# The end of a mixer + MoE decode kernel: norm rows loaded with h, the last down product by column halves, the mean from an accumulated output, sample rows over 128 partitions

## The chip, the cores and the metric

The kernel runs on 1 core of one Trainium2 chip. The metric is the device time of one execution in microseconds (us). Before the change it is 1081.07 us, the median of 3 runs (1079.88 to 1082.58).

## What is computed

One decoder layer in fp32 on 512 prompt tokens and 8 sample tokens, 520 in all, each of 1024 features. A three-branch token mixer and a first LayerNorm give `h`. Then, cut from the reference:

```
f = sum over e of gates[:, e] * ((silu(h @ w_gate[e]) * (h @ w_up[e])) @ w_down[e])   # 16 experts, top 2 per token
y = layer_norm(ALPHA * h + f, ln2_g, ln2_b)
layer_norm(x) = (x - mean) * rsqrt(mean((x - mean)^2) + 1e-5) * g + b                 # over the 1024 features
```

Each token has two experts with weights that add up to one. The outputs are `y` for the prompt, `y` for the samples, and the convolution states, which are done long before the end.

## The kernel before

The five engines run programs written by hand, each in the order in which it is written, and meet at semaphores. Nothing is reordered by a scheduler. The names below are those of the code: `pe` is TensorE, `act` ScalarE, `dve` VectorE, `pool` GpSimd, `sp` the queue on SyncE from which most DMAs are issued. On each engine `settle()` is a wait of the engine for its own last result.

The mixer takes the first 740 us. Then the 16 experts follow, step `m` = 0 to 15 (in the order of `TURN`), each on up to 96 tokens (`C`) that are gathered to one tile. fp32 matrices are split into a rounded part and a remainder, so that each product takes three passes: `act` writes the rounded weights into `ring` (L764), `dve` subtracts them to get the remainder (`low_parts`, L1497), and `pe` multiplies hi by hi, hi by lo, lo by hi (`product`, L1076). A step of `pe` is: gate product, up product (both to 512 columns), and the down product of the expert before (to 1024 columns in two halves of 512, each in a PSUM bank of its own), 24 matmuls of 512 columns each. A step of `dve` holds the 12 remainders of the three matrices and four smaller things. After each down product `act` copies 96 rows of 1024 from PSUM to `y_out` (`rows_out`, L805) and `sp` stores them in the DRAM table `y_rows` (`store`, L444).

Where a token's two rows stand in that table comes from the routing. `find_slots` (L1569) works it out for each of the two choices, on tiles of 128 partitions x 5 token blocks: block 0 to 3 are the prompt, block 4 holds the 8 samples, so that 8 partitions of it are in use. It runs on `dve` at the ends of the steps m = 13 and m = 14. `order_slots` (L1580) orders the two, in step m = 15, in the middle of the remainders of the up matrix.

The end goes through these steps:

- `load_back` (L446): when the down product of m = 13 is done, `sp` loads `h` back from DRAM (`h_back`). The rows of gain and bias of the last norm (`load_rows`, `ln2_rows`) are loaded after the store of m = 14.
- `fetch` (L600): `pool` gathers for each of the five blocks the row of the earlier expert (`y_a`), as soon as the slots are known and 12 experts are stored. After the last store has landed, `sp` signals `y_read` (L517), and `pool` gathers the rows of the later expert (`y_b`).
- `partials` (L1597) on `dve`: y_a = y_a * weight + h_back, five blocks, after `h_back` and the norm's rows have landed.
- `summed_up(b)` (L1625): y_a = y_b * weight + y_a (L1629), then `bn_stats` on two halves (L1631) and `bn_aggr` (L1633) for mean and variance.
- `act` takes the root of the variance, 128 x 1 (L862).
- `normalise(b)` (L1635): (y_a - mean) * g (L1638), a reciprocal of the root (L1640), and times that plus the bias row (L1642). Then `sp` stores the block (L523).

`dve` runs `summed_up(0)`, and then for b = 1 to 4 `summed_up(b)` and `normalise(b - 1)`, and `normalise(4)`. The last product, `down_last` (L1086), takes the four chunks of 128 rows one after the other and in each both column halves, so that both halves end together.

Of the kernel before, what the change touches and what calls it, by code (L numbers as in the profile page):

```python
# [30 lines left out]
P = 128  # L31
# [82 lines left out]
def build(nc, x_prompt, x_sample, state_conv_a, state_conv_b, w_in, conv_a_w, w_a_out, conv_b_w, conv_b_bias,  # L114
# [16 lines left out]
    with ExitStack() as ctx:  # L131
# [61 lines left out]
        h_back = place("h_back", "X_HI", [P, NTB, D], plus=NTB * D * 4)  # L193
        y_b = place("y_b", "Q_HI", [P, NTB, D])
        ln2_rows = place("ln2_rows", "Q_HI", [P, 2, D], plus=NTB * D * 4)
# [32 lines left out]
        s_max, s_sum, s_w1, s_w2, s_ps, s_t, s_slot, s_slot2 = (sb(f"s{i}", [P, NTB]) for i in range(8))  # L228
# [9 lines left out]
        hs = place("hs", "tail_b", [C, D])  # L238
        y_out = place("y_out", "b_pad", [C, D], plus=6 * NTB * E * 4)
# [15 lines left out]
        stats = sb("stats", [P, 2, 2, 6])  # L255
# [8 lines left out]
        const_ready, spatial_masked, pool_chain = sem("const_ready"), sem("spatial_masked"), sem("pool_chain")  # L264
# [11 lines left out]
        mean_rounded, x_mean_ready, z_ready, sq_ready, h_white = (sem(n) for n in ("mean_rounded", "x_mean_ready", "z_ready", "sq_ready", "h_white"))  # L276
        wo_in = [sem(f"wo_in{j}") for j in range(4)]
        wo_centred, rw_b_ready, rw_ready, b_ready = sem("wo_centred"), sem("rw_b_ready"), sem("rw_ready"), sem("b_ready")
        tok_var, tok_std, diag_ready, r_spread = sem("tok_var"), sem("tok_std"), sem("diag_ready"), sem("r_spread")
        lg_transposed, table_ready = sem("lg_transposed"), sem("table_ready")  # L280
# [20 lines left out]
        lg_turned, lg_ready = sem("lg_turned"), sem("lg_ready")  # L301
        loads_begun, gathers_begun = sem("loads_begun"), sem("gathers_begun")
# [5 lines left out]
        fin_out = [sem("fin_out0"), sem("fin_out1")]  # L308

        MATRICES = ("gate", "up", "down")  # L310

        class Pass:


            def __init__(self, tag):
# [10 lines left out]
                self.stored = sem(tag + "stored")  # L326
# [8 lines left out]
                "meanB": (centred, 2), "varB": (std_ready, 2), "meanX": (x_mean_ready, 1), "biasL": (b_ready, 1),  # L335
# [47 lines left out]
        def _(sp):  # L383
# [4 lines left out]
            def load(slot, n, view, col):  # L388
                sp.wait_ge(w_split, n * 2 + 2)
                sp.sem_inc(loads_begun, 1)  # L390
                sp.dma_start(raw[:, slot], view[:, :, bass.ds(col, P)]).then_inc(raw_in[slot], 16)
# [59 lines left out]
            def load_rows():  # L451
# [414 lines left out]
        def _(pe):  # L866
# [271 lines left out]
            with pe.Else():  # L1138
                pe.nop()
# [535 lines left out]
```

## Time and profile before

| | us |
|---|---|
| median of 3 runs | 1081.07 |
| the profiled execution's own time | 1081.94 |
| its span in the trace | 1079.9 |
| PE busy | 997.7 (92%) |
| DVE busy | 807.4 (75%) |
| ACT busy | 472.1 (44%) |
| POOL busy | 344.5 (32%) |
| end of the last matmul | 1040.6 |
| the first `y_b` is used | 1051.18 |

The busy times are of the whole span and say little of its end: the last 39 us, 3.6% of the span, hold no matmul. TensorE's granted clock is at full speed up to its last matmul. The trace counts from the start of the profiled execution, whose own time is 2.0 us longer than its span.

### The profile page before, as it was taken

The page shows a single profiled execution, that of the slowest core. Times are in us where ns is not written, and L with a number is a line of the kernel's source. Part 1 is how long each engine was busy: PE and PEld are TensorE (multiplying, and loading weights), DVE is VectorE, ACT ScalarE, POOL GpSimd, SP SyncE. Part 2 cuts the span into 40 slices and gives each one's busy share as a digit, 9 for nine tenths or more (in the row PEclk, how much of TensorE's full clock was granted, in tenths as well). Part 3 has the DMA queues.
Part 4 walks back from the last instruction along what each step waited for, and adds up shares of the span by engine and source line. Part 5 has one row for each costly group of instructions (what it writes and reads, how often), then busy time and mean ns, then how long its engine had stood idle before and what let it go on. Part 6 is the DMA issues. An engine that isn't in the chain of part 4 may idle for free.

```text
span 1079.9 us, 19395 instructions
## 1 busy us (share of the span) xinstructions
PE 997.7 (92%) x7175; PEld 902.5 (84%) x7175; DVE 807.4 (75%) x986; ACT 472.1 (44%) x657; POOL 344.5 (32%) x268
## 2 busy tenths in 40 slices
PE   6999999999999899999999998986999999999950
PEld 5999999999999798999999998964677777777630
DVE  2398889888898976744335596147889898989969
ACT  3222322322322144334442322245787878787820
POOL 2444444444544241445445443410200000000060
PEclk9999999999999899999999998996999999999985
DMA  7423332332332221332334524457999999999562
GB/s 202 121 86 92 97 89 86 97 94 81 97 96 61 78 78 49 97 114 79 97 97 156 175 78 156 157 198 269 337 371 377 390 385 389 385 389 344 186 200 108
DMA packets 162375, 189.91 MB, mean 176 GB/s; under 512 B 5875, under 2 KB 113395, under 8 KB 162316
## 3 DMA queue, kind: packets, MB, share of 16 engines
q1 hardware_dynamic: 155819, 177.46, 48.4%
q0 software_dynamic: 3008, 10.55, 3.1%
q10 hardware_dynamic: 3505, 1.36, 0.5%
q8 instruction: 24, 0.39, 0.2%
q14 instruction: 19, 0.16, 0.0%
HBM read 178.57 MB, written 11.76 MB: 176 GB/s over the span
## 4 chain that ended last, share of the span: by engine, by line
PE 51%; issue 28%; POOL 12%; DVE 4%; DMA 2%; ACT 2%; POOLq 0%; DVEq 0%; ACTq 0%
PE pr L915 26%; PE pr L1076 14%; POOL w_lo L546 10%; PE work L1076 7%; DMA hs<-h_rows,ids 2%; PE work L1062 1%; POOL y_a L603 1%; PE work L985 1%; DVE stats L1631 1%; DVE y_a L1629 1%; ACT h_f L773 1%; DVE y_b L1638 1%; PE work L1037 1%; DMA y_b<-y_rows,slot_b 0%; PE pr L1093 0%
## 5 line engine op out<-in xcount | busy, mean ns | idle before, releaser
L546 POOL TENSOR_TENSOR w_lo<-raw,w_hi 128x512 fp32r<-128x512 f32 x208 | 281.6, 1373 | 365.3 <-ACT w_hi L631 365.3
L915 PE MATMUL pr<-x_hi,w_hi 128*128 128x260 f32 x1280 | 259.7, 284 | 3.1 <-POOL w_lo L546 3.1
L915 PE MATMUL pr<-x_hi,w_lo 128*128 128x260 f32 x1280 | 259.0, 284 | 0.0
L915 PE MATMUL pr<-x_lo,w_hi 128*128 128x260 f32 x1280 | 258.9, 284 | 0.0
L635 ACT ACTIVATE ev<-pr 128x520 f32<-128x520 f32 x96 | 58.2, 606 | 389.2 <-PE pr L915 389.2
L915 PEld LDWEIGHTS pr<-x_hi,w_hi 128*128 128x128 f32 x1280 | 199.0, 190 | 3.5 <-DVE x_lo L1183 3.3
L915 PEld LDWEIGHTS pr<-x_hi,w_lo 128*128 128x128 f32 x1280 | 198.5, 190 | 0.0
L915 PEld LDWEIGHTS pr<-x_lo,w_hi 128*128 128x128 f32 x1280 | 198.2, 190 | 0.0
L1235 DVE SCALAR_TENSOR_TENSOR work<-b_pad,par,work 128x512 f32<-128x512 f32 x224 | 148.1, 744 | 0.0
L631 ACT ACTIVATE w_hi<-raw 128x512 fp32r<-128x512 f32 x208 | 118.9, 622 | 5.5 <-DMA raw<-in_w_in_dram 3.2
L1076 PE MATMUL pr<-ring,hs_hi 128*96 128x512 f32 x256 | 103.0, 403 | 4.1 <-DVE hs_lo L1503 2.0
L582 POOL DMA_INDIRECT hs<-h_rows,ids x16 | 20.1, 1259 | 256.2 <-DVE ids L1491 215.9
L1076 PE MATMUL pr<-ring,hs_lo 128*96 128x512 f32 x256 | 101.5, 396 | 0.0
L1497 DVE TENSOR_TENSOR w_up_lo<-w_up,ring 128x1024 fp32r<-128x1024 f32 x64 | 75.5, 1221 | 21.9 <-ACT ring L764 21.8
L1497 DVE TENSOR_TENSOR w_gate_lo<-w_gate,ring 128x1024 fp32r<-128x1024 f32 x64 | 75.2, 1214 | 3.7 <-ACT ring L764 3.5
L764 ACT ACTIVATE ring<-w_gate 128x1024 fp32r<-128x1024 f32 x64 | 67.4, 1060 | 21.1 <-PE pr L1076 12.1
L1497 DVE TENSOR_TENSOR w_down_lo<-w_down,ring 128x1024 fp32r<-128x1024 f32 x64 | 75.2, 1216 | 0.0
L1290 DVE TENSOR_TENSOR ev<-ev,ev 128x520 f32<-128x520 f32 x16 | 11.9, 743 | 79.9 <-ACT ev L635 79.9
L764 ACT ACTIVATE ring<-w_down 128x1024 fp32r<-128x1024 f32 x64 | 65.7, 1054 | 8.1 <-PE pr L1076 8.1
L764 ACT ACTIVATE ring<-w_up 128x1024 fp32r<-128x1024 f32 x64 | 62.4, 1047 | 3.4 <-PE pr L1076 3.4
L1076 PEld LDWEIGHTS pr<-ring,hs_hi 128*96 128x96 f32 x256 | 41.8, 163 | 22.6 <-DVE hs_lo L1503 2.3
L1076 PEld LDWEIGHTS pr<-ring,hs_lo 128*96 128x96 f32 x256 | 41.8, 163 | 18.3
(279 smaller groups left out, 1675.9 us busy)
## 6 DMA issues: line engine op xcount, KB each, us to landing
raw<-in_w_in_dram SPq DMA_DIRECT2D x80, 512.0 KB, 3.7
w_gate<-in_expert_w_gate_dram SPq DMA_DIRECT2D x16, 2048.0 KB, 14.6
w_up<-in_expert_w_up_dram SPq DMA_DIRECT2D x16, 2048.0 KB, 13.7
w_down<-in_expert_w_down_dram SPq DMA_DIRECT2D x16, 2048.0 KB, 13.3
y_rows<-y_out SPq DMA_DIRECT2D x16, 384.0 KB
raw<-in_w_a_out_dram SPq DMA_DIRECT2D x8, 512.0 KB, 3.6
raw<-in_w_c_out_dram SPq DMA_DIRECT2D x8, 512.0 KB, 3.6
raw<-in_w_b_out_dram SPq DMA_DIRECT2D x8, 512.0 KB, 3.6
```

The source lines that it names most:

```text
L546: pool.tensor_tensor(w_lo[:, slot, k], raw[:, slot, k], w_hi[:, slot, k].bitcast(F32), ALU.subtract).then_inc(w_split, 1)
L582: pool.indirect_dma_start(out=hs[:], out_offset=None, in_=h_rows, in_offset=bass.IndirectOffsetOnAxis(ap=ids[:, m % 2:m % 2 + 1], axis=0)) ...
L603: pool.indirect_dma_start(out=dst[0:n, b, :], out_offset=None, in_=table, in_offset=bass.IndirectOffsetOnAxis(ap=slot[0:n, b:b + 1], axis= ...
L631: act.activation(w_hi[:, slot, k], raw[:, slot, k], ACT.Copy).then_inc(w_rounded, 1)
L635: act.activation(out, src[:, :, 0:HALF], func).then_inc(evacuated, 1)
L764: act.activation(rounded(kind, i, last), chunk(kind, s, i), ACT.Copy).then_inc(ps.hi[kind], 1)
L773: act.activation(h_f[:, k, :], h_f[:, k, :], ACT.Identity, scale=par[:, k * NROWS + R_L1G:k * NROWS + R_L1G + 1], bias=par[:, k * NROWS + ...
L915: mm = pe.matmul(pr[slot][:, h, 0:HALF], w[:, slot, k, :], x[:, k, h * HALF:(h + 1) * HALF], start=(k == 0 and w is w_hi and x is hi), sto ...
L1076: mm = pe.matmul(out(h), x[:, k, :], w[:, cols], start=(k == 0 and x is hi and w is w_hi_i), stop=(k == k_of * CH - 1 and x is lo))
L1235: do(dve.scalar_tensor_tensor(acc, b_pad[:, k:k + TP], col(j, R_CONVB + k), acc, ALU.mult, ALU.add))
L1290: do(dve.tensor_tensor(gate[:], gate[:], prod[:], ALU.mult))
L1497: dve.tensor_tensor(chunk(kind, s, i, w_e_lo), chunk(kind, s, i), rounded(kind, i, last).bitcast(F32), ALU.subtract).then_inc(ps.lo_dve[ki ...
```

## The change

1. **Norm rows.** `ln2_rows` moves to the memory of expert slot 1, beside `h_back`, and is loaded in `load_back`. For the samples a second copy of gain and bias is laid out by 16 small loads of 16 partitions x 64.
2. **Slots.** `find_slots` works out both choices together and runs once, at m = 13; a compare with a table `kc` and one sum replace a loop over the passes. `order_slots` moves from m = 15 to the end of m = 14 and also prepares the 5 columns `s_own` for the samples.
3. **Samples over 128 partitions.** The 8 rows of 1024 are treated as 128 rows of 64. `pool` builds two masks after its last gather of tokens; `pe` spreads `s_own` from 8 to 128 partitions by a matmul in the middle of the down product of m = 14; `spread_samples` on `dve` copies it and makes indices, after its last remainders; each gather of samples waits for that. Mean and variance of a sample are put together over 16 partitions by two matmuls with `block_mean`.
4. **Last down product by halves.** All four chunks of columns 0 to 511 first, then 512 to 1023. `act` copies each half as it is done to a buffer of its own, `sp` stores each by itself. `pool` waits for the stores itself, without `y_read`.
5. **Mean and variance.** L1744 writes the sum of its output to `agg` as it goes (`accum_out`), a small multiply turns it into minus the mean, and `act` squares (`Square` with that as bias, also summed as it goes) and takes the root. `bn_stats` and `bn_aggr` are gone. The samples come between the prompt's blocks, and prompt block 3 is the last.

The rest are semaphores that are merged with others. The core of the diff:

```diff
@@ sp: load_back, the last stores
-                sp.dma_start(h_back[0:TS, 4, :], h_rows[TP:T, :]).then_inc(back_in, 16)
+                sp.dma_start(sh_back, h_rows[TP:T, :].rearrange("s (c f) -> (s c) f", f=CS)).then_inc(back_in, 16)
+                for i, row in enumerate((ln2_g, ln2_b)):
+                    sp.dma_start(ln2_rows[:, i, :], row[0].partition_broadcast(P)).then_inc(ln_in, 16)
+                    for s in range(TS):
+                        k = P // TS
+                        sp.dma_start(sln2[s * k:(s + 1) * k, i, :], row[0].rearrange("(c f) -> c f", f=CS)).then_inc(ln_in, 16)
+            def store_last(ps, q, row0):
+                x = E - 1
+                sp.wait_ge(ps.half_ready, q + 1)
+                sp.dma_start(y_rows[bass.ds(x * C + row0, C), 0:D // 2], y_last[:, 0:D // 2]).then_inc(ps.half_stored, 16)
+                sp.wait_ge(ps.y_ready, q * E + (E + 1))
+                sp.dma_start(y_rows[bass.ds(x * C + row0, C), D // 2:D], y_last[:, D // 2:D]).then_inc(ps.stored, 16)
@@ pool: after the last token gather
+            def fetch_samples(dst, which, landed, table):
+                pool.indirect_dma_start(out=dst, out_offset=None, in_=table.rearrange("r (c f) -> (r c) f", f=CS),
+                                        in_offset=bass.IndirectOffsetOnAxis(ap=s_idx[:, which:which + 1], axis=0)).then_inc(landed[4], 16)
             fetch(y_a, slot_early, y_a_in, y_rows[0:EARLY * C, :])
+            pool.wait_ge(sample_dve, 2)
+            fetch_samples(sy_a, 0, y_a_in, y_rows[0:EARLY * C, :])
...
             with pool.Else():
-                pool.wait_ge(y_read, 1)
+                pool.wait_ge(first.half_stored, 16)
+                pool.wait_ge(first.stored, 16 * (E + 1))
                 fetch(y_b, slot_b, y_b_in, y_rows[0:E * C, :])
+                fetch_samples(sy_b, 2, y_b_in, y_rows[0:E * C, :])
@@ act
+            def last_rows_out(ps, t):
+                act.wait_ge(ps.done["down"], t * CH + CH + 2)
+                act.activation(y_last[:, 0:512], work[0][0:C, 0, :], ACT.Copy).then_inc(ps.half_ready, 1)
+                act.wait_ge(ps.done["down"], t * CH + 2 * CH)
+                act.wait_ge(ps.stored, t * 16 + 16)
+                act.activation(y_last[:, 512:1024], work[0][0:C, 1, :], ACT.Copy).then_inc(ps.y_ready, 1)
+            def deviation(b):
+                s = b % 2
+                act.wait_ge(var_ready, b + 1)
+                act.activation(pr[0][:], y_a[:, b, :].rearrange("p (h n) -> p h n", h=2), ACT.Square, bias=agg[:, s, 1:2],
+                               accum_out=agg[:, s, 2:3]).then_inc(std2_ready, 1)
+                act.wait_ge(std2_ready, 2 * b + 1)
+                act.activation(agg[:, s, 3:4], agg[:, s, 2:3], ACT.Sqrt, scale=1.0 / D, bias=eps_t[:, 1:2]).then_inc(std2_ready, 1)
@@ dve: expert_pass
-                    if ps is first and m == E - 1:
-                        order_slots()
...
                     if ps is first and m == 13:
-                        find_slots(oh1, s_slot)
+                        find_slots()
                     if ps is first and m == 14:
-                        find_slots(oh2, s_slot2)
+                        order_slots()
@@ dve: the end
-                step(dve.scalar_tensor_tensor(y_a[0:n, b, :], y_b[0:n, b, :], s_wb[0:n, b:b + 1], y_a[0:n, b, :], ALU.mult, ALU.add))
-                for h in range(2):
-                    do(dve.bn_stats(stats[0:n, s, h, :], y_a[0:n, b, h * 512:(h + 1) * 512]))
+                step(dve.scalar_tensor_tensor(y_a[:, b, :], y_b[:, b, :], s_wb[:, b:b + 1], y_a[:, b, :], ALU.mult, ALU.add,
+                                              accum_out=agg[:, s, 0:1]))
+                do(dve.tensor_scalar(agg[:, s, 1:2], agg[:, s, 0:1], -1.0 / D, None, ALU.mult), to_var)
```

Where the change moves instructions, at three places. First `dve` in the last expert step (m = 15), before; the rows ahead of it are `find_slots`, which ends in eleven instructions on 128x5, each waiting for the one before. `w_up_lo` are remainders of the up matrix, `s_...` the small tiles of the slots:

```order
L1578 TENSOR_TENSOR s_144<-s_144,s_142 128x5
L1497 TENSOR_TENSOR w_up_lo_86<-w_up_77,ring 128x1024 x2
L1582 TENSOR_TENSOR s_142<-s_143,s_144 128x5
L1583 TENSOR_TENSOR s_137<-s_140,s_142 128x5
...
L1594 TENSOR_SCALAR s_142<-s_142 128x5
L1595 CAST slot_early<-s_142 128x5
L1497 TENSOR_TENSOR w_up_lo_86<-w_up_77,ring 128x1024 x2
L1497 TENSOR_TENSOR w_down_lo_91<-w_down_82,ring 128x1024 x2
L1517 TENSOR_TENSOR u_lo<-pr,u_hi 128x384
```

and the same place now (`s_own`, `s_pos` belong to the slots, too):

```order
L1588 TENSOR_TENSOR w_gate_lo_83<-w_gate_74,ring 128x1024 x2
L1679 TENSOR_TENSOR s_151<-s_pair 128x5
...
L1697 CAST slot_early<-s_pos 128x5
L1698 TENSOR_TENSOR s_own<-s_pos,id_cols 8x1
L1588 TENSOR_TENSOR w_up_lo_86<-w_up_77,ring 128x1024 x4
L1588 TENSOR_TENSOR w_down_lo_91<-w_down_82,ring 128x1024 x2
L1608 TENSOR_TENSOR u_lo<-pr,u_hi 128x384
```

The slots' order now takes the place of the second `find_slots`, and the four remainders of the up matrix follow each other with nothing between them.

Second the queue of `sp`, from the load of `h` to the last store, before:

```order
L448 DMA h_back<-h_rows 128x4x1024
L449 DMA h_back<-h_rows 8x1024
L444 DMA y_rows<-y_out 96x1024
L452 DMA ln_rows<-in_ln_g_dram 128x1024
L453 DMA ln_rows<-in_ln_b_dram 128x1024
```

and now (the 16x64 loads are the samples' copy of gain and bias):

```order
L459 DMA h_back<-h_rows 128x4x1024
L460 DMA h_back<-h_rows 128x64
L462 DMA ln_rows<-in_ln_g_dram 128x1024
L465 DMA h_back<-in_ln_g_dram 16x64 x8
L462 DMA ln_rows<-in_ln_b_dram 128x1024
L465 DMA h_back<-in_ln_b_dram 16x64 x8
L455 DMA y_rows<-y_out 96x1024
```

Eighteen loads stand ahead of the store of m = 14 that stood behind it or were not there.

Third the end on `dve`, one block in the middle, before:

```order
L1629 SCALAR_TENSOR_TENSOR y_a<-y_b,s_138,y_a 128x1024
L1631 BN_STATS stats<-y_a 128x6 x2
L1633 BN_AGGR agg<-stats 128x2
L1638 SCALAR_TENSOR_TENSOR y_b<-y_a,agg,ln_rows 128x1024
L1640 RECIPROCAL agg<-agg 128x1
L1642 SCALAR_TENSOR_TENSOR y_a<-y_b,agg,ln_rows 128x1024
```

and the last rows now (`s_agg` and 128x64 are the samples):

```order
L1764 SCALAR_TENSOR_TENSOR y_a,s_agg<-y_b,s_spread,y_a 128x64
L1744 SCALAR_TENSOR_TENSOR y_a,agg<-y_b,s_147,y_a 128x1024
L1746 TENSOR_SCALAR agg<-agg 128x1
L1751 SCALAR_TENSOR_TENSOR y_b<-y_a,agg,ln_rows 128x1024
L1753 RECIPROCAL agg<-agg 128x1
L1755 SCALAR_TENSOR_TENSOR y_a<-y_b,agg,ln_rows 128x1024
L1769 SCALAR_TENSOR_TENSOR y_b<-y_a,s_agg,h_back 128x64
L1771 RECIPROCAL s_agg<-s_agg 128x1
L1773 SCALAR_TENSOR_TENSOR y_a<-y_b,s_agg,h_back 128x64
L1751 SCALAR_TENSOR_TENSOR y_b<-y_a,agg,ln_rows 128x1024
```

and on `act`, where `pr` is only a place to write the squares:

```order
L923 ACTIVATE pr,agg<-y_a,agg 128x1024
L926 ACT_TABLE_LOAD
L926 ACTIVATE agg<-agg,eps_t 128x1
L923 ACTIVATE pr,agg<-y_a,agg 128x1024
L926 ACTIVATE agg<-agg,eps_t 128x1
```

Two passes over 512 columns each left `dve`, one over 1024 came to `act`, and the table load that stood ahead of all roots stands behind the first square.

## Rows read from the trace of the kernel before

**Rows 1.** Busy time by stretch: from:to us, length, busy us and count per engine, PEclk, DMA.
```profile
1040.62:1051.18 10.56, 0.00 (x0) 0.00 (x0) 6.11 (x5) 2.30 (x2) 4.47 (x4) 0.74 0.55 174
1051.18:1077.72 26.54, 0.00 (x0) 0.00 (x0) 26.02 (x35) 1.47 (x5) 1.74 (x2) 0.50 0.34 130
```
**Rows 2.** Timeline of DVE from 1051 us: start, us, engine, line, operation, tiles.
```profile
1051.18 1.28 DVE L1629 SCALAR_TENSOR_TENSOR y_a<-y_b,s,y_a 128x1024 f32<-128x1024 f32 x1 [0.81 <-DMA y_b<-y_rows,slot_b]
1052.50 1.29 DVE L1631 BATCH_NORM_STATS2 stats<-y_a 128x6 f32<-128x512 f32 x2
1053.82 0.21 DVE L1633 BATCH_NORM_AGGREGATE agg<-stats 128x2 f32<-128x12 f32 x1
1053.95 1.24 DVE L1629 SCALAR_TENSOR_TENSOR y_a<-y_b,s,y_a 128x1024 f32<-128x1024 f32 x1
...
1056.67 1.23 DVE L1638 SCALAR_TENSOR_TENSOR y_b<-y_a,agg,ln_rows 128x1024 f32<-128x1024 f32 x1
...
1059.21 1.28 DVE L1629 SCALAR_TENSOR_TENSOR y_a<-y_b,s,y_a 128x1024 f32<-128x1024 f32 x1
...
1076.45 1.27 DVE L1642 SCALAR_TENSOR_TENSOR y_a<-y_b,agg,ln_rows 8x1024 f32<-8x1024 f32 x1
```
**Rows 3.** Timeline of POOL from 1031 us.
```profile
1031.07 6.38 POOL L603 DMA_INDIRECT y_a<-y_rows,slot_early  x1 [0.30 <-issue]
1045.80 1.77 POOL L603 DMA_INDIRECT y_b<-y_rows,slot_b  x1 [8.35 <-SPq L517]
1047.88 0.94 POOL L603 DMA_INDIRECT y_b<-y_rows,slot_b  x1 [0.30 <-issue]
```
**Rows 4.** Timeline of SP's queue.
```profile
963.19 2.37 SPq L444 DMA_DIRECT2D y_rows<-y_out  x1
...
1017.12 0.89 SPq L449 DMA_DIRECT2D h_back<-h_rows  x1
...
1041.70 0.35 SPq L444 DMA_DIRECT2D y_rows<-y_out  x1
```
**Rows 5.** Waits of SP's queue from 980 us: total us, times, longest.
```profile
SPq L513 <- DMA y_rows<-y_out: 3.3, 1, 3.3
```
**Rows 6.** Timeline of PE, last expert's product.
```profile
1028.88 0.47 PE L1076 MATMUL work<-ring,u_hi 128*96 128x512 f32 x1 [0.87 <-DVE u_lo L1517]
...
1040.22 0.40 PE L1076 MATMUL work<-ring,u_lo_last 128*96 128x512 f32 x1
```
**Rows 7.** Waits from 980 us: total us, times, longest.
```profile
PE pr L1076 <- DVE w_up_lo L1497: 1.1, 1, 1.1
```
**Rows 8.** Timeline of DVE around the slots, and its last remainders.
```profile
1016.58 0.23 DVE L1570 TENSOR_TENSOR router<-router,e_off 128x80 f32<-128x80 f32 x1
...
1019.64 2.36 DVE L1497 TENSOR_TENSOR w_up_lo<-w_up,ring 128x1024 fp32r<-128x1024 f32 x2
1021.92 0.15 DVE L1582 TENSOR_TENSOR s<-s,s 128x5 f32<-128x5 f32 x1
...
1023.73 2.36 DVE L1497 TENSOR_TENSOR w_up_lo<-w_up,ring 128x1024 fp32r<-128x1024 f32 x2
...
1034.35 2.35 DVE L1497 TENSOR_TENSOR w_down_lo<-w_down,ring 128x1024 fp32r<-128x1024 f32 x2
```
**Rows 9.** Timeline of ACT from 1040 us.
```profile
1040.65 1.02 ACT L805 ACTIVATE y_out<-work 96x1024 f32<-96x1024 f32 x1 [4.53 <-PE work L1076]
1044.74 1.28 ACT L862 ACT_TABLE_LOAD   x1 [3.07 <-issue]
1054.07 0.29 ACT L862 ACTIVATE agg<-agg,eps_t 128x1 f32<-128x1 f32 x1 [8.04 <-DVE agg L1633]
```
**Rows 10.** Groups of ACT's instructions: busy us, mean ns, idle before.
```profile
L756 ACT ACTIVATE ev<-m 128x520 f32<-128x520 f32 x8 | 5.1, 638 | 41.7 <-DVE m L1394 41.7
```
**Rows 11.** DMA issues: KB each, median us to landing.
```profile
out_dram<-y_a SPq DMA_DIRECT2D x4, 512.0 KB, 2.6
```
**Rows 12.** Tile `y_b`: from issue to landing.
```profile
DMA to landing us min/median/max: 5.0/5.4/6.0
```

More of the change, by code:

```diff
@@ L842, in expert_pass @@
                 rows_out(ps, t - 1)
[L843 removed]
+                last_rows_out(ps, t)
             act.sem_inc(first.silu_ready, 1)
@@ L1087, in down_last @@
                 pe.wait_ge(ps.u_lo_ready, t + 1)
-                product(ps, "down", 0, t, u_hi_last, u_lo_last, lambda h: work[0][0:C, h, :], 2, last=True)
+                for h in range(2):
+                    for k in range(CH):
+                        if h == 0:
+                            pe.wait_ge(ps.lo_dve["down"], t * CH + (k + 1))
+                        cols = slice(h * 512, (h + 1) * 512)
+                        w_lo_k, w_hi_k = chunk("down", 0, k, w_e_lo), rounded("down", k, True)
+                        for x, w in ((u_hi_last, w_hi_k), (u_hi_last, w_lo_k), (u_lo_last, w_hi_k)):
+                            mm = pe.matmul(work[0][0:C, h, :], x[:, k, :], w[:, cols], start=(k == 0 and x is u_hi_last and w is w_hi_k),
+                                           stop=(k == CH - 1 and x is u_lo_last))
+                    mm.then_inc(ps.done["down"], 2)
             def turn_u(ps, t):
@@ L1120, in expert_pass @@
                 turn_u(ps, t)
+                if ps is first:
+                    pe.wait_ge(const_ready, 6)
+                    pe.wait_ge(sample_dve, 1)
+                    pe.matmul(pr[1][:, 1, 8:13], spread[:], s_own[:], start=True, stop=True).then_inc(sample_mm, 1)
                 down(ps, (E - 2) % 3, t - 1, chunks=(2, 3))
@@ new lines, in order_slots, with spread_samples @@
+                do(dve.tensor_copy(slot_early[:], s_pos[:, 0, :]), to_slots)
+                do(dve.tensor_tensor(s_own[:, 0:1], s_pos[0:TS, 0, 4:5], own, ALU.subtract), Tally(dve, sample_dve, 0))
+                last[0] = chain
+            def spread_samples():
+                last[0] = chain
+                dve.wait_ge(sample_mm, 1)
+                step(dve.tensor_copy(s_spread[:], pr[1][:, 1, 8:13]))
+                dve.scalar_tensor_tensor(s_idx[:], s_spread[:, 0:3], float(P // TS), id_cols[:, 0, 1:2].to_broadcast([P, 3]), ALU.mult,
+                                         ALU.add).then_inc(sample_dve, 1)
@@ new lines, in summed_up, with normalise @@
+                do(dve.tensor_scalar(agg[:, s, 1:2], agg[:, s, 0:1], -1.0 / D, None, ALU.mult), to_var)
+            def normalise(b):
+                s = b % 2
+                to_var.wait(0 if b == 3 else 1)
+                do(dve.scalar_tensor_tensor(y_b[:, b, :], y_a[:, b, :], agg[:, s, 1:2], ln2_rows[:, 0, :], ALU.add, ALU.mult))
+                dve.wait_ge(std2_ready, 2 * b + 2)
+                do(dve.reciprocal(agg[:, s, 3:4], agg[:, s, 3:4]))
+                settle()
+                do(dve.scalar_tensor_tensor(y_a[:, b, :], y_b[:, b, :], agg[:, s, 3:4], ln2_rows[:, 1, :], ALU.mult, ALU.add), to_fin)
@@ L1644, in _ @@
             last[0] = chain
             summed_up(0)
-            for b in range(1, NTB):
-                summed_up(b)
-                normalise(b - 1)
-            normalise(NTB - 1)
+            summed_up(1)
+            normalise(0)
+            summed_up(2)
+            normalise(1)
+            dve.wait_ge(y_b_in[4], 16)
+            do(dve.scalar_tensor_tensor(sy_a, sy_b, s_spread[:, 4:5], sy_a, ALU.mult, ALU.add, accum_out=s_agg[:, 0:1]), Tally(dve, sample_dve, 2))
+            last[0] = chain
```

231 lines of the change are left out of this document (142 added, 89 removed).

## The prediction, made before the changed kernel was run

> **What bounds the end of the kernel now.** I read the page's chain of waits first, then the busy time by stretch, then the timelines of DVE, POOL, SP and PE over the last 60 us. The change touches nothing that is on the chain before the last two expert steps, so the first 1015 us stay. After that the chain has four pieces.
>
> (a) PE runs to 1040.62, where its last matmul ends [rows 6]. It is almost full, but it waits twice in the last expert step, 1.1 us for a remainder of the up matrix [rows 7] and 0.87 us for `u_lo` [rows 6]. Both come from DVE, and in front of both DVE has worked on slots: 3.06 us of `find_slots` from 1016.58 to 1019.64, and 1.81 us of `order_slots` from 1021.92 to 1023.73 [rows 8].
>
> (b) Then there is a relay with almost no work in it, 10.56 us without a matmul [rows 1]. ACT copies the last 96 x 1024 rows in 1.02 us [rows 9], SP issues the store at 1041.70 [rows 4], waits 3.3 us for it to land [rows 5], signals POOL, which starts the first gather at 1045.80 [rows 3], and DVE gets the rows at 1051.18 [rows 2]: 5.4 us after the issue. What DVE does meanwhile (the partial sums) is off the chain.
>
> (c) DVE is then the bound for 26.54 us, 26.02 of them busy [rows 1]. A block costs 1.32 for L1629, 1.32 for the two `bn_stats`, 0.13 for `bn_aggr` and 2.54 for `normalise` (from 1056.67 to 1059.21), 5.3 us in all, five times [rows 2]. The fifth block has 8 rows and costs the same: its last instruction takes 1.27 us on 8 partitions, as the others do on 128 [rows 2]. The time goes by columns, not by rows.
>
> (d) From 1077.72, the end of that instruction, to the span's end at 1079.9 the last store of 32 KB takes 2.2 us.
>
> **The change, part by part.**
>
> Slots and PE. `find_slots` had 15 instructions in 3.06 us, 0.20 each, and runs twice. The joint one has 12, so about 2.4 us, once, and `order_slots` grows from 14 in 1.81 us (0.13 each) to 19, about 2.5 us. DVE saves 7.9 - 4.9 = 3.0 us, and what counts more, it starts the up remainders of the last step at 1016.6 + 2.5 = 1019.1 and does all four in one go, so the second pair starts at 1021.4, not at 1023.73 [rows 8]. PE's two waits go, 1.1 + 0.9, with some 0.1 for the slow first matmul behind each. The next thing that could be late is `u`, the input of the last product. DVE's order after the slots is the old one without 1.8 us, and PE comes 1.1 to 2.0 us earlier, so DVE keeps its lead. The matmul that spreads `s_own` is new on PE; its data are ready since 1019, I put 0.15 us. Net -2.0 us: the last matmul ends at 1038.6. Bounds: 0 (DVE is late elsewhere) and -2.2. The order by halves needs the fourth chunk's remainders 2.1 us after the product's start instead of 4.1. The start would be about 1032.9, so at 1035.0; DVE ends them at about 1034.4 (below). It fits with little to spare.
>
> Store and relay. ACT copies half the columns, about 0.55 us instead of 1.02 [rows 9]. The first half is done and stored 2.8 us earlier, beside the matmuls. SP's issue then stands at 1038.65 + 0.58 = 1039.2. The store before took 3.7 us from its issue (0.35 + 3.3), while the two norm rows, 1 MB, were on the same queue; a 512 KB store at the end lands in 2.6 us [rows 11]. I take 2.6 for 192 KB with nothing beside it, bounds 2.0 and 3.7. POOL waits itself, which saves some 0.3 of the 0.4 us between 1045.4 and 1045.80. So the gather can start at 1039.2 + 2.6 + 0.1 = 1041.9 instead of 1045.80: -3.9 us, of which 2.0 are PE's.
>
> POOL before that. The gathers of `y_a` start 4 us earlier and end before 1033. The samples' gather waits for `spread_samples`, behind DVE's last remainders. These ended at 1036.7 [rows 8], 17.1 us after 1019.64 with 1.8 us of slots among them; now 1019.1 + 15.3 = 1034.4, and 0.3 for the spread. The samples' gather before, the fifth of its row, took POOL 6.38 us where others take 0.94 [rows 3]. If that goes with its place it comes again: 1034.7 + 6.4 = 1041.1, and some 0.5 us for reading the count and branching, 1041.6. This is just ahead of 1041.9, so I cost it at nothing, but its cover is 0.3 us thick. The masks are built right after the last gather of tokens, more than one expert step before PE wants them.
>
> SP. Eighteen more loads stand ahead of the store of m = 14. The queue issued the samples' `h` at 1017.12, and that takes 0.89 us [rows 4]; at about 0.5 us each the 18 end near 1027. The store of m = 14 is due near 1034. Hidden. DVE's partial sums, held up to 1044.27 by the norm rows, run from about 1035 and are done near 1042, before `y_b` is there.
>
> The tail on DVE. T is the landing of the first `y_b`: 1041.9 + 5.4 = 1047.3, where it was 1051.18 [rows 2, 3].
> - `summed_up` becomes 1.32 + the read-out of the accumulator + 0.13 for the multiply (as `bn_aggr`). No row shows DVE writing an accumulated output. The lower bound is 0; the upper is that the sum costs a second pass as long as `bn_stats`, 1.32. I take 0.1, near the cost of the small instructions, so 1.55 us.
> - The second block's `y_b` was issued 2.08 us after the first and takes 5.4 [rows 3, 12], so it lands at T + 2.1, after the first `summed_up` is done (T + 1.55). This wait of 0.55 us was hidden by `bn_stats` and is new. `summed_up(1)` ends at T + 3.65.
> - ACT for block 0: square from T + 1.55. 520 columns of Square take 0.64 [rows 10]; scaled to 1024 at most 1.26. Table load 1.28, root 0.29 [rows 9], 0.1 for hops: T + 4.5. DVE wants the root 1.15 us into `normalise`, T + 4.8. Hidden by 0.3 us. Later blocks need no load, and ACT has 4 us per block for 1.7 us.
> - Blocks: four `summed_up`, 6.2; four `normalise`, 10.16; the wait, 0.55; the samples, one sum (0.25, as the 0.23 us of a 128x80 instruction [rows 8]) and a short `normalise` (0.6). Sum 17.8 us in place of 26.54: -8.7.
> - The samples' way over PE and ACT (two small matmuls, copy, square, root) starts at T + 10.5 and ends near T + 12.5; DVE needs it at T + 14.6, and the last block's root at T + 16.3. Hidden.
>
> The last store now has 512 KB. It lands 2.6 us after its issue [rows 11], and the end follows about 0.5 later: 3.1 instead of 2.2, +0.9.
>
> **A rule that speaks against one step.** The trace shows the table load as 1.28 us [rows 9], and the root could start right behind it. The Trainium skill, "ScalarE: Activation LUTs", section "What ACT_TABLE_LOAD costs", adds about 1.38 us of drain to each load. No row here shows a drain behind the load, since it was over 8 us before its root. By the page the first root would come at T + 5.9 and DVE would stand 1.1 us. The same skill's "VectorE: DVE Perf Modes", section "Two Vector instructions with no wait between them", counts an operation that also writes its accumulator as two instructions; it gives no price.
>
> **Sum.** -3.9 (first gather) - 8.7 (DVE) + 0.9 (last store) = -11.7 us. The span of 1079.9 becomes 1068.2. The profiled execution, 1081.94 with 2.0 us around its span, becomes 1070.2. It stands 0.9 above the median, so the median goes from 1081.07 to 1069.4.
>
> **Rivals.**
> - The fifth gather's 6.38 us is no matter of place but falls on a `y_b` gather, or the samples' gather starts later than I think (for: the row, and the thin cover; against: only one of ten gathers showed it). It moves T by up to 5.4: 1074.8.
> - PE gains nothing, since DVE is late for the last product's remainders instead, now wanted 2 us sooner: +2.0, 1071.4.
> - The accumulated sum costs DVE a second pass (for: nothing here bounds it; against: the two inputs are read once in 1.28 us, and a sum over the output needs no second reading). Four times 1.2: 1074.2.
> - The drain behind the table load, a wait of DVE in block 0: +1.1, 1070.5.
> - The slower side: SP's queue. Its issues take 0.35 to 0.89 us when it is empty, but one took 2.37 us behind 2 MB loads [rows 4]. The new loads stand right behind the 2 MB of `h_back`. At x us each the queue is free at 1019 + 18x, wanted at 1034 to 1036. Up to x = 0.9 nothing is lost. The whole gain is gone at (1035.5 + 11.7 - 1019)/18 = 1.6 us each. At 2.37 us each it would be free at 1061.7, 26 us late: 1069.4 + 26 = 1095.6. Against it: the 2.37 us stood behind several loads of 2 MB, here there is one, the issue right behind it took 0.89 us, and the small loads are 4 KB each.
>
> **How the numbers follow.** My forecast 60%, POOL 12%, PE 8%, accumulated sum 8%, drain 6%, SP 6% (4% beyond break-even or near it, 2% only dear). The errors of my own case are about 2 us to each side: the landing of the half store (2.0 to 3.7), the first gather's issue (1.77 or 0.94), the read-outs (0 to 0.2, five times). With the rivals up to the POOL case the range is 1065.5 to 1074.8; outside are SP's case and sums of two rivals, and more than I allow for on the fast side. A change under 0.3% (3.2 us) can't be told from none here. Faster 95%, within it 2%, slower 3%.
>
> **What would show it.** PE's last matmul near 1038.6 and no wait of PE over 0.3 us in the last step. POOL's first `y_b` gather at 1041.9 with the half store as releaser; if it starts right behind the samples' gather, the cover was too thin. DVE's gaps in the tail: 0.5 us before the second `summed_up`, none before the first reciprocal. The distance from L1744 to the multiply behind it gives the price of the accumulated sum. SP's last norm load before 1030. I am wrong if the stretch from the first `y_b` to DVE's last instruction is over 20 us or the first `y_b` lands after 1049.

## The result and the profile after

The changed kernel takes 1068.32 us, the median of 4 runs (1066.08 to 1072.0), against 1081.57 (1079.88 to 1082.58) for the kernel before on the same chip. The ratio is 0.9875, with a 95% interval of 0.9853 to 0.9898. The difference is -13.25 us, forecast was -11.7. The profiled execution took 1067.2 us, its span is 1065.5.

First the chain of waits from the copy of the expert before (m = 14) to the landing of the second `y_b`, for which DVE's second block waits: start, us, what the time went to.

```profile
1029.34 1.04 ACT y_out L859
...
1030.39 6.20 DMA y_rows<-y_out
...
1036.68 0.60 ACT y_last L866
1037.28 0.02 issue
1037.30 2.38 DMA y_rows<-y_last
...
1039.72 0.73 issue
1040.45 1.13 POOL y_b L642
1041.58 0.30 issue
1041.89 5.11 DMA y_b<-y_rows,slot_b
```

PE is not on this piece of the chain. Its last matmul, here in PE's timeline, ends at 1034.87, and ACT's copy of the second half starts at 1036.68 only:

```profile
1034.47 0.40 PE L1169 MATMUL work<-ring,u_lo_last 128*96 128x512 f32 x1
```

The waits say what held the copy (total us, times, longest). It is the store of m = 14, the expert before:

```profile
POOL y_b L642 <- DMA y_rows<-y_last: 8.2, 1, 8.2
ACT y_last L866 <- DMA y_rows<-y_out: 4.0, 1, 4.0
DVE y_a L1744 <- DMA y_b<-y_rows,slot_b: 3.4, 2, 3.0
```

The two waits of PE in the last step [rows 6, 7] are gone, no wait of PE for DVE's remainders is left there. The slots, seen in DVE's timeline, answer to [rows 8]: `order_slots` takes 1.98 us (forecast 2.5), and the four remainders of the up matrix follow in one go.

```profile
1012.99 0.15 DVE L1679 TENSOR_TENSOR s<-s_pair 128x5 f32<-128x5 f32 x1
...
1014.90 0.14 DVE L1698 TENSOR_TENSOR s_own<-s_pos,id_cols 8x1 f32<-8x1 f32 x1
1014.97 4.61 DVE L1588 TENSOR_TENSOR w_up_lo<-w_up,ring 128x1024 fp32r<-128x1024 f32 x4
```

The first blocks on DVE answer to [rows 2]:

```profile
1045.12 1.28 DVE L1744 SCALAR_TENSOR_TENSOR y_a<-y_b,s,y_a 128x1024 f32<-128x1024 f32 x1 [2.96 <-DMA y_b<-y_rows,slot_b]
1046.33 0.08 DVE L1744 DVE_READ_ACCUMULATOR y_a<-y_b,s,y_a 128x1 f32 x1
1046.45 0.15 DVE L1746 TENSOR_SCALAR agg<-agg 128x1 f32<-128x1 f32 x1
1047.02 1.28 DVE L1744 SCALAR_TENSOR_TENSOR y_a<-y_b,s,y_a 128x1024 f32<-128x1024 f32 x1 [0.42 <-DMA y_b<-y_rows,slot_b]
...
1049.61 0.15 DVE L1753 RECIPROCAL agg<-agg 128x1 f32<-128x1 f32 x1
1049.80 1.28 DVE L1755 SCALAR_TENSOR_TENSOR y_a<-y_b,agg,ln_rows 128x1024 f32<-128x1024 f32 x1
...
1059.36 0.16 DVE L1771 RECIPROCAL s_agg<-s_agg 128x1 f32<-128x1 f32 x1
...
1061.14 1.28 DVE L1755 SCALAR_TENSOR_TENSOR y_a<-y_b,agg,ln_rows 128x1024 f32<-128x1024 f32 x1
```

The accumulated sum is a row of its own, 0.08 us; nothing stands before the first reciprocal. ACT beside it, as [rows 9]:

```profile
1046.64 1.12 ACT L923 ACTIVATE pr<-y_a,agg 128x1024 f32<-128x1024 f32 x1 [9.37 <-DVE agg L1746]
1047.69 0.19 ACT L923 ACTIVATION_READ_ACCUMULATOR pr<-y_a,agg 128x1 f32 x1
1047.90 1.28 ACT L926 ACT_TABLE_LOAD   x1
1049.19 0.29 ACT L926 ACTIVATE agg<-agg,eps_t 128x1 f32<-128x1 f32 x1
```

The stretch from the first `y_b` to DVE's last instruction by busy time, columns as in [rows 1], where it was 26.54 us:

```profile
1045.12:1062.42 17.30, 1.17 (x4) 1.00 (x4) 16.56 (x29) 8.08 (x17) 1.80 (x2) 0.50 0.44 171
```

**Where a profile starts to count.** One trace differs from the next by more than most of these steps. I therefore take as zero the first gate matmul of the last step (m = 15) and measure from there. All us, each from the timelines of one profiled execution:

| kernel | zero at | zero to PE's end | to first `y_b` gather | to its first use | DVE's stretch | end | zero to end |
|---|---|---|---|---|---|---|---|
| before | 1015.00 | 25.62 | 5.18 | 5.38 | 26.54 | 2.18 | 64.90 |
| changed | 1011.34 | 23.53 | 5.58 | 4.67 | 17.30 | 3.08 | 54.16 |
| changed, again | 1015.06 | 23.52 | 6.06 | 4.56 | 17.39 | 3.01 | 54.54 |
| mean and variance alone | 1010.07 | 25.86 | 5.37 | 4.59 | 20.75 | 2.16 | 58.73 |
| slots alone | 1015.24 | 23.05 | 5.74 | 5.38 | 26.55 | 2.24 | 62.96 |
| halves alone | 1011.78 | 25.76 | 5.75 | 5.08 | 26.54 | 2.19 | 65.32 |
| norm rows alone | 1014.31 | 25.63 | 5.39 | 4.55 | 26.54 | 2.18 | 64.29 |
| changed, copy doesn't wait | 1012.73 | 23.52 | 4.15 | 4.74 | 17.69 | 3.07 | 53.17 |
| masks early | 1012.92 | 23.52 | 5.63 | 4.79 | 17.67 | 3.07 | 54.68 |
| copy doesn't wait and masks early | 1015.33 | 23.49 | 3.80 | 4.77 | 17.21 | 3.10 | 52.37 |
| changed without samples' part | 1012.73 | 23.03 | 3.99 | 4.79 | 20.82 | 2.24 | 54.87 |
| two wide loads | 1014.38 | 23.53 | 5.75 | 5.58 | 17.33 | 3.03 | 55.22 |
| two wide loads, no wait | 1013.98 | 23.52 | 4.17 | 4.87 | 17.60 | 3.06 | 53.22 |
| longer program, no wait | 1009.58 | 23.55 | 4.85 | 4.51 | 17.64 | 3.07 | 53.62 |

The zero lies between 1009.6 and 1015.3. Most of this spread arises long before the end: POOL's first gather of tokens, behind the mixer, starts anywhere from 735.1 to 739.9 us in the same fourteen profiles. The pieces behind the zero repeat within some 0.5 us, with a scatter of up to 1 us in the relay and in the landing of the first `y_b`. So 10.7 of the 14.4 us between the first two profiles lie behind the zero, and 3.7 stand ahead of it.

In the repetition, too, the store of m = 14 and then the second half's store make up the chain. It gives other sizes for them (start, us, what the time went to):

```profile
1034.11 5.55 DMA y_rows<-y_out
...
1040.35 3.52 DMA y_rows<-y_last
```

### The profile page after: what moved, and what is told of

Its sections match the earlier page's. It is cut to its first block, busy times and chain, and to the rows that moved or that the text cites. A ratio compares the mean times of both kernels' runs of the same rounds, so it can differ in the third digit from the quotient of the medians.

```text
span 1065.5 us, 19424 instructions
## 1 busy us (share of the span) xinstructions
PE 996.4 (94%) x7181; PEld 902.0 (85%) x7181; DVE 793.6 (74%) x969; ACT 477.3 (45%) x669; POOL 357.7 (34%) x275
## 4 chain that ended last, share of the span: by engine, by line
PE 55%; issue 26%; POOL 11%; DVE 3%; DMA 2%; ACT 2%; POOLq 0%; DVEq 0%; ACTq 0%
PE pr L989 27%; PE pr L1150 16%; POOL w_lo L567 11%; PE work L1150 8%; PE work L1136 1%; PE work L1059 1%; DMA y_rows<-y_out 1%; PE pr L1176 1%; ACT h_f L827 1%; DMA y_b<-y_rows,slot_b 0%; DVE y_b L1751 0%; PE work L1111 0%; DMA hs<-h_rows,ids 0%; PE work L1035 0%; DVE y_a L1744 0%
## 6 DMA issues: line engine op xcount, KB each, us to landing
w_down<-in_expert_w_down_dram SPq DMA_DIRECT2D x16, 2048.0 KB, 13.2
y_rows<-y_out SPq DMA_DIRECT2D x15, 384.0 KB, 12.9
```

## The experiments

**Four of the five parts, each alone.** Each takes the lines of one part of the change into the kernel before (the code is shortened). The fifth, the samples' part, is taken out of the changed kernel further down.

```diff
# mean and variance alone
-step(dve.scalar_tensor_tensor(y_a..., ALU.mult, ALU.add)); bn_stats x2; bn_aggr
+step(dve.scalar_tensor_tensor(y_a..., ALU.mult, ALU.add, accum_out=agg[0:n, s, 0:1]))
+do(dve.tensor_scalar(agg[0:n, s, 1:2], agg[0:n, s, 0:1], -1.0 / D, None, ALU.mult), to_var)
# act: Square with accum_out, then Sqrt
# slots alone
-find_slots(oh1, s_slot) at m=13, find_slots(oh2, s_slot2) at m=14, order_slots() in m=15
+find_slots() at m=13, order_slots() at m=14
# halves alone
-store(first, E - 1, E - 1, 0)
+store_last(first, 0, 0)      # with down_last by halves, last_rows_out, pool's own waits
# norm rows alone
 load_back()
+load_rows()                  # ln2_rows beside h_back, before the store of m=14
```

Mean and variance alone:

> The kernel before with part 5 alone (sum written by L1744's counterpart, squares and root on ACT); five blocks as before. Theory: DVE's bn_stats and bn_aggr leave the path, 5 x 1.3 us, less 0.5 us of waiting for the second y_b: DVE's last stretch 26.5 -> 20.5 us, time -6.0 us. Rival (ACT's square and table load stand in the way block by block): 23 us or more, -3.5 or less.

1075.59 us against 1080.98, ratio 0.9951 (0.9934 to 0.9967). DVE's stretch fell from 26.54 to 20.75. From zero to the end it is 6.2 us less, more than half of the change's 10.7.

Slots alone:

> The kernel before with part 2 alone (joint find_slots, order_slots at m = 14, without s_own). Theory: PE's waits for DVE in the last step go, the last matmul comes 2.1 us earlier counted from the end of the down product of m = 13, and the time falls by 2.1 us. Rival: the y_a gathers, now 4 us earlier, run beside the store of m = 14 and lengthen it, so that the last copy on ACT waits for that store and the time falls by under 1 us.

1078.76 us, ratio 0.9978 (0.9956 to 0.9999). PE ends 2.57 us earlier after the zero; the relay behind gives 0.6 back, so that 1.9 are left. The rival does not show: the `y_a` gathers are all issued by 1028.0 here, 5.8 us ahead of the store of m = 14, and ACT's last copy starts 0.04 us after PE's end.

Halves alone:

> The kernel before with part 4 alone (last down product by column halves, two stores, POOL waits for the stores itself), with the semaphores merged to make room. Theory: copy -0.45, store of 192 KB instead of 384 KB -0.3 to -1.0, no hop over SP -0.3: first y_b use 1.0 to 1.8 us earlier after the last matmul. Rival: the norm rows still run beside the store, which keeps its 3.7 us: -0.7.

1082.89 us, ratio 1.0012 (0.9989 to 1.0034). No gain. SP's queue and POOL in the timelines of this kernel:

```profile
1033.44 0.89 SPq L453 DMA_DIRECT2D ln_rows<-in_ln_g_dram  x1
1034.37 0.46 SPq L454 DMA_DIRECT2D ln_rows<-in_ln_b_dram  x1
1036.25 0.36 SPq L460 DMA_DIRECT2D y_rows<-y_last  x1
1038.19 0.33 SPq L462 DMA_DIRECT2D y_rows<-y_last  x1
```
```profile
1043.29 1.53 POOL L613 DMA_INDIRECT y_b<-y_rows,slot_b  x1 [8.93 <-DMA y_rows<-y_last]
```

The second half is issued at 1038.19, 0.65 us after PE's end, where the whole store before was issued 1.08 after it [rows 4, 6]. But POOL gets going 5.1 us later: the half store takes 4.32 us to land, and POOL starts 0.78 behind that. Two norm rows (1 MB) and the first half are issued ahead of it. In the profiles of the changed kernel and its variants, where the norm rows are long there, the same store takes 2.37 to 3.52 us. That the norm rows are what makes it 4.32 is not shown, and the next run speaks against a simple form of it.

Norm rows alone:

> The kernel before with part 1 alone (the two norm rows of 512 KB loaded right after h, without the samples' copies). Theory: the last store no longer has 1 MB beside it and lands 2.6 to 3.0 us after its issue, not 3.7: -0.7 to -1.1 us. Rival: the landing is fixed cost, 0.

1080.1 us, ratio 0.9986 (0.9967 to 1.0005). From zero to the end 0.6 us less. The theory failed all the same. The last store has no norm row beside it now and lands no sooner: SP waits 3.5 us for it, where it was 3.3 [rows 5].

```profile
SPq L513 <- DMA y_rows<-y_out: 3.5, 1, 3.5
```

The gain is in the step from the first `y_b` gather to its use, 4.55 for 5.38. DVE's partial sums are now done early, and it waits 5.9 us for `y_b` instead of 0.8 [rows 2]. The relay was the chain, not the partial sums.

**The changed kernel once more, and two suspects.** The copy of the second half writes columns of `y_last` that nothing has read in the first pass, so its wait for the store of m = 14 can go there. The masks can be built while POOL waits for the second step.

```diff
# copy doesn't wait
-                act.wait_ge(ps.stored, t * 16 + 16)
+                if ps is further:
+                    act.wait_ge(ps.stored, t * 16 + 16)
# masks early: the masks' block moves from behind the last token gather
+                    if m == 0 and ps is first:
+                        build_masks()
```

Again, unchanged:

> The changed kernel again, unedited, as the measure for the others of this group. Its profile: if the 3.7 us by which the first profile of it was ahead before the last two expert steps belong to the run and not to the change, this profile has another value there (0 to 4 us ahead of before), and the stretch from the end of the down product of m = 13 to the end is again 54.0 us (64.7 before).

1068.58 us against 1081.75, ratio 0.9861 (0.9835 to 0.9887). As expected, the head start was the run's: the zero stands at 1015.06, where it was 1015.00 before the change. From there to the end it is 54.54, 0.4 more than in the first profile.

Copy doesn't wait:

> The changed kernel, but ACT's copy of the last half no longer waits for the store of m = 14 (in the first pass; the half goes to a buffer that this store does not read). Theory A (that wait alone costs): the copy starts at PE's end, 1.8 us earlier, and so does all behind it: -1.8 us. Theory B (the DMA queues are busy with the y_a gathers until 2 us after PE's end): the half store lands later after its issue than 2.4 us and takes back 1 us or more: -0.8 us or less.

1067.59 us, ratio 0.9853 (0.9829 to 0.9878). ACT's timeline of this kernel:

```profile
1036.28 0.59 ACT L867 ACTIVATE y_last<-work 96x512 f32<-96x512 f32 x1 [2.18 <-PE work L1170]
```

The copy is released by PE. The first gather comes 1.4 to 1.9 us earlier after PE's end, and from zero to the end it is 1.0 to 1.4 us less, between the two theories. The half store lands in 2.73 us. The times can't tell this version from the changed one.

Masks early:

> The changed kernel, but POOL builds the two masks between its third and fourth gather of tokens, some 230 us earlier. Theory (POOL stalls some 6 us when it goes from one kind of work to another): the first y_a gather takes 2 us, not 7.4, all y_a gathers end 5 us earlier, the store of m = 14 has less beside it and lands in 3 to 4 us, not 6.2, and ACT no longer waits for it: -1.8 us. Rival (the stall goes by time or by the number of gathers): 6 us again in one of the y_a gathers, no gain.

1069.4 us, ratio 0.9877 (0.985 to 0.9903): no change, and POOL's first `y_a` gather took 7.43 us as before. The expectation that it goes with the masks failed. The store of m = 14 takes 5.28 us and still holds the copy, by 0.9 us.

Both:

> Both edits: masks early and no wait of ACT for the store of m = 14. If both remove the same wait, -1.8 us as each alone, not -3.6; if the y_a gathers also slow the half store, some tenths more than without the masks' move.

1070.17 us, ratio 0.9881 (0.9856 to 0.9906). From zero to the end this is the shortest, 52.37, but its zero stood at 1015.33. What the tail gains is within the scatter of what stands ahead of it. The two edits don't add up: the masks alone had gained nothing.

**Without the samples' part.** The changed kernel with `h_back[0:TS, 4]`, `y_a` and `y_b` of 8 rows, a fifth block of `summed_up` and `normalise`, and none of `sln2`, `spread`, `block_mean`, `s_own`.

> The changed kernel without its third part: the 8 samples stay on 8 partitions as a fifth block of 8 x 1024, without the sixteen small norm loads, masks, spread matmul and sample indices. Theory (each part pays for itself in the stretch where it stands): DVE's stretch from the first y_b to its last instruction is 17.3 in the changed kernel; its sample instructions (about 0.85 us there) become a full block of 4.0, so 20.4 to 20.8, and the last store shrinks to 32 KB (end 2.2 instead of 3.1). From the start of the last step's gate product to the end of the span 54.16 becomes 56.4, the time 2.3 us longer than the changed kernel. Rival: the sample gather, the masks and small loads cost nothing either way elsewhere; if they do hold POOL or the queue, the difference is under 1.5 us. On POOL's long first y_a gather (7.43 us): if the sixteen small loads cause it, it is gone here; if the two rows of 512 KB do, it stays.

The ratio is 0.9885 (0.9847 to 0.9923). From zero to the end it is 54.87, only 0.3 to 0.7 us more than the changed kernel, where 2.3 were expected. DVE's stretch is 3.4 to 3.5 longer and the end 0.8 shorter, as expected, but PE ends 0.5 earlier, and the gather comes 1.6 to 2.1 us earlier after that. POOL in the timeline of this kernel:

```profile
1016.08 1.82 POOL L617 DMA_INDIRECT y_a<-y_rows,slot_early  x1 [27.04 <-DVE slot_early L1637]
1018.20 1.95 POOL L617 DMA_INDIRECT y_a<-y_rows,slot_early  x1 [0.30 <-issue]
1020.46 1.96 POOL L617 DMA_INDIRECT y_a<-y_rows,slot_early  x1 [0.30 <-issue]
1022.72 0.94 POOL L617 DMA_INDIRECT y_a<-y_rows,slot_early  x1 [0.31 <-issue]
```

and of the changed kernel:

```profile
1015.27 7.43 POOL L642 DMA_INDIRECT y_a<-y_rows,slot_early  x1 [19.09 <-DMA y_rows<-y_out]
1023.00 2.41 POOL L642 DMA_INDIRECT y_a<-y_rows,slot_early  x1 [0.30 <-issue]
1025.72 2.56 POOL L642 DMA_INDIRECT y_a<-y_rows,slot_early  x1 [0.30 <-issue]
1028.58 2.43 POOL L642 DMA_INDIRECT y_a<-y_rows,slot_early  x1 [0.30 <-issue]
1031.32 0.95 POOL L647 DMA_INDIRECT y_a<-y_rows,s_idx  x1 [0.30 <-issue]
```

Without the samples' part POOL has issued all five gathers by 1025.1, and the store of m = 14 (issued at 1031.29, landed 2.9 us later) has no gather being issued beside it. With it they go on to 1032.3, into the store issued at 1030.39, which then needs 6.20 us and holds the second half's copy. In the other three profiles with both the part and the wait this store needs 5.26 to 5.55 us. No run changes the gathers alone, so that they are what lengthens it is the likely reading, not a shown one. In the kernel without the part that copy is released by PE:

```profile
1035.80 0.59 ACT L831 ACTIVATE y_last<-work 96x512 f32<-96x512 f32 x1 [2.18 <-PE work L1124]
```

Two things follow from the table. The relay is 3.99 us here and was 5.18 before, while slots, halves and norm rows alone had 5.74, 5.75 and 5.39: these parts shorten it only together. And the samples' part saves 0.3 to 0.7 us as long as the copy waits, but 1.7 (54.87 to 53.17) where it doesn't.

**What makes POOL slow there.** Two edits, in three kernels.

```diff
# two wide loads instead of sixteen small ones
-for s in range(TS):
-    sp.dma_start(sln2[s * k:(s + 1) * k, i, :], row[0].rearrange("(c f) -> c f", f=CS)).then_inc(ln_in, 16)
+every = bass.AP(chunks.tensor, chunks.offset, [[0, TS], [CS, P // TS], [1, CS]])
+sp.dma_start(sln2[:, i, :], every).then_inc(ln_in, 16)
# longer program
+for _ in range(16):
+    chain.inc(pool.memset(spread[:], 1.0)); chain.wait()
```

Two wide loads:

> The changed kernel with the sixteen small loads of the samples' gain and bias put into two DMAs (each reads the row eight times, once per sample, to 128 partitions x 64). Theory (the small loads only occupy SP's queue, 0.5 us each, and it is empty long before it is wanted): SP's last norm load at about 1016.5 instead of 1023.8, everything behind unchanged, from the start of the last step's gate product to the end 54.2 within 0.4, time the same within 1.5 us. Rival (the many small loads in flight are what POOL's first y_a gather of 7.43 us stands behind): that gather takes under 2.5 us and the y_a gathers end 5 us earlier; the store of m=14 then has no gather beside it and lands in under 4 us instead of 6.2, so that the second half's copy doesn't wait for it: tail about 52.5, 1.8 us shorter.

1070.56 us against 1082.01, ratio 0.9889 (0.9867 to 0.9911). SP's queue is through its norm loads at 1020.6, 4.6 us after the load of `h_back`, where the small ones took 10.8. From zero to the end it is 55.2, 1.0 more than the theory had, with 3.50 us for the half store and 5.58 from the first gather to its use: no gain, and the stall stays:

```profile
1017.74 7.42 POOL L642 DMA_INDIRECT y_a<-y_rows,slot_early  x1 [18.84 <-DVE slot_early L1697]
```

Two wide loads, and the copy doesn't wait:

> As the last, and the copy of the second half doesn't wait for the store of m=14 in the first pass (it writes a buffer of its own that nothing has read yet). Theory: tail 53 as with the wait alone taken away, some 1 us below the changed kernel, time 1067 to 1068. Rival (the small loads stand behind POOL's long gather): the half store also has fewer gathers beside it and lands 0.5 us sooner, tail 52.3 or less.

1068.28 us, ratio 0.987 (0.9848 to 0.9892). The tail is 53.2, as without the wait alone. The small loads cost the path nothing.

The longer program, and the copy doesn't wait:

> The changed kernel with the copy of the second half not waiting for the store of m=14, and with sixteen more writes of the 8x128 mask on POOL ahead of the two masks (each with a wait for the one before), so that POOL's program is 32 instructions longer ahead of the y_a gathers; they run while POOL is idle, after the last gather of tokens. Theory P (POOL's stalls of 6.3 to 7.4 us belong to places in its program, where code has to be brought in): the stall of 7.4 us leaves the first y_a gather for another instruction, most likely one of the new writes or a mask; the y_a gathers then take 1.8 to 2.0 us each as without the samples' part, and end 5 us earlier, with the store of m=14 landing sooner. Theory Q (the stall belongs to the first y_a gather, by what is in flight there): it takes 7.4 us again and the tail from the last step's gate product is 53.2 as without the wait alone. Either way the half store's landing sets the first y_b gather, so the tail is 52.7 to 53.3 and the time 1067 to 1068.

1067.49 us against 1080.42, ratio 0.9884 (0.9858 to 0.991), and in POOL's timeline the same gather again:

```profile
985.73 3.98 POOL L625 MEMSET spread<- 8x128 f32 x16
...
990.04 3.14 POOL L629 TENSOR_SCALAR_AFFINE_SELECT spread<-spread 8x128 f32<-8x128 f32 x1
...
1013.76 7.43 POOL L645 DMA_INDIRECT y_a<-y_rows,slot_early  x1 [19.26 <-DMA y_rows<-y_out]
```

So the stall did not leave this gather when 32 instructions were put ahead of it. From zero to the end it is 53.6, 0.3 above the range expected, with 3.43 us for the half store. The stall of 7.43 us comes with the samples' part; neither the sixteen loads, nor the masks' place, nor the length of POOL's program brings it. The part is not the only thing that moves such stalls: before the change one of 6.38 us stood at the fifth `y_a` gather [rows 3], and with slots alone no `y_a` gather has one. What of the samples' part brings it (the 128x64 load of the samples' `h` is a piece not tried) stays open.

## Why the prediction was right, and where it was not

The forecast of 1069.4 us lies 1.1 us above the measured median. Most of the mechanism held: PE's waits went, DVE's end was shortened by what the working had for it. The relay did not, and that the total came out so close is partly luck. In the terms of the sum, from the table above:

- **PE, -2.0.** It is -2.1. Slots alone gave -2.6, and the samples' part takes 0.5 of it back: the kernel without it has PE's end at 23.03. I had put 0.15 for the spreading matmul. No remainder was late for the product by halves.
- **Store and relay, -1.9 beside PE's part: this step failed.** I had 3.3 us from PE's end to the first gather (1038.6 to 1041.9); it is 5.6 to 6.1, more than the 5.2 before. The landing came out near in this profile (2.38 us for 2.6). What failed is "SP's issue then stands at 1038.65 + 0.58". ACT's copy also waits for the store of m = 14, a line of the diff that my working passed over, and that store needs 6.20 us. The copy starts 1.8 us after PE's end there, 0.9 to 1.2 in the other three profiles with the wait, and taking the wait away gives 1.4 to 1.9 back. The rest, 0.5 net of the quicker landing, is POOL, which starts 0.77 us after it where I had 0.1. Before, SP's wait for the store ended at 1045.35 (1041.70 + 0.35 + 3.3) and POOL started 0.45 later [rows 3, 4, 5]: POOL's own wait lost 0.3 us where I had it save 0.3. The landing of 2.38 us that I had sized so well is one profile's, too; in the repetition it is 3.52. So the last product by halves gained nothing as changed, and nothing alone.
- **POOL before that.** The four gathers of the prompt were to end before 1033, 18 us after the zero. They end 19.7 after it, and only the early zero of this profile makes that 1031.0. The first took 7.43 us and the samples' 0.95, not the other way round: the stall is tied to neither the fifth gather nor the samples' one. The last is issued 20.9 us after the zero, so the cover before the first `y_b` was 8 us and not 0.3. That it did not fall on a `y_b` gather keeps the first rival out.
- **Landing to use, 5.4.** It is 4.7. The first gather itself took 1.13 us instead of 1.77 [rows 3].
- **DVE, -8.7.** It is -9.2. The stretch is 17.30 for 17.8 forecast. The wait before the second block is 0.42 (forecast 0.55), the accumulated sum 0.08 (0.1), `summed_up(0)` from the start of L1744 to the end of the multiply 1.48 (1.55). By experiment 5.8 of it are mean and variance, 3.4 to 3.5 the samples.
- **Last store, +0.9.** It is +0.9. In the account of the samples' part it cancels a quarter of what DVE gains.
- **SP's queue.** The small loads took 0.46 to 0.59 us each, and the queue was free at 1023.8. The slower rival needed 1.6 each.

From zero to the end this is -2.1 + 0.4 - 0.7 - 9.2 + 0.9 = -10.7 where I had -11.7. The measured -13.25 is 2.5 more; the interval of the ratio reaches down to -11.0. The repetition gave -10.4 from zero to the end. The remainder must stand ahead of the last step, but for 0.1 to 0.3 us outside the span. The zero moves by 5.7 us from profile to profile, so one profile of each can't say whether the change moves it too (its median over the five profiles without the slots' and mean's code together is 1014.3, over the nine with them 1012.9). The spans of all runs say more. Less the tail of each kernel's own profile, they put the zero at 1014.7 on average in 60 runs of the kernel before and at 1013.2 in 40 of the changed kernel and its variants. That is an estimate, since the tail was profiled once or twice per kernel and scatters by up to 1 us, but it makes some 1.5 us of the remainder look like the change's own. I had said that the first 1015 us stay; what in them would gain is open. So the total came out closer than the worst of its steps: the miss of 2.3 us in the relay was covered by small gains elsewhere and by this remainder, neither of which was forecast.

The other rivals: the accumulated sum has no second pass (0.08 us, not 1.3). The drain behind the table load doesn't show: the load starts at 1047.90, takes 1.28, and the root starts at 1049.19. The Trainium skill, "ScalarE: Activation LUTs", section "What ACT_TABLE_LOAD costs", adds about 1.38 us of drain to each load; by it the root would start at 1050.6 (an estimate from that figure). The measurement decides: here the load costs its own 1.28 us. On the accumulated output the Trainium skill, "VectorE: DVE Perf Modes", section "Two Vector instructions with no wait between them", counts two instructions, and the trace agrees, with a second row of 0.08 us.

**The version that the experiments point to.** The changed kernel with the copy not waiting: 1067.59, 1068.28 (with wide loads) and 1067.49 us (with a longer program) in three measurements, each against its own runs of before 14.2, 13.7 and 12.9 us faster. A fourth, with the masks early, is 1070.17 us, 11.6 faster. The changed kernel itself is 13.2 us faster twice. From zero to the end the four are 0.5 to 2.2 us shorter than its two profiles, but the times don't resolve that.

## What to carry to other kernels

When a chain is shortened at its head, read each wait of the instruction that moves: a semaphore that was long past before (here a store of the step before) can be the last to come now, and transfers that an earlier step has set free run right into it. A part that gains on the busiest engine is to be charged with what it adds elsewhere: the samples over 128 partitions took 3.4 to 3.5 us from DVE and gave 0.5 back on PE, 0.8 at the last store and 1.6 to 2.1 in the relay. And where the start of the interesting stretch moves by 5 us from profile to profile, fix a zero inside the program and compare from there.

## What the runs showed of the hardware

- Accumulated outputs appear as a row of their own: 0.08 us on DVE (128x1024 and 128x64 alike), 0.19 us on ACT.
- The 192 KB store of the second half lands in 2.37 to 3.52 us in nine profiles without norm rows beside it and in 4.32 with halves alone. The 384 KB store of m = 14 lands in 2.9 us with no gather being issued beside it and in 5.26 to 6.20 us in the four profiles in which gathers were still being issued and the copy waited for it.
- A gather on POOL takes 0.9 to 2.6 us, but single ones 6.3 or 7.4 us, at the same place and within 0.02 us the same: the fourth gather of tokens in every kernel (6.28); the fifth of `y_a` before [rows 3] and with mean and variance, halves or norm rows alone (6.38); the first of `y_a` in every kernel with the samples' part (7.43); none of `y_a` with slots alone or without the samples' part. The masks of 8x128 are less regular: in the first profile of the changed kernel they took 7.18 and 0.28 us, in the second 4.01 and 3.10. The cause is open.
- POOL starts its first `y_b` gather 0.77 us after the landing that it waits for; before, by way of SP's signal, it was 0.45.
